# Expert passes in another order, and a context mixer's output turns and closing norms moved into the stages after the experts

## What is computed

```python
# end of the first block: 32 experts (4 groups of 8, top 2 of one group), then the final norm
x = x + gt2 * hier_moe(modulate(rms_norm(x, norm2_g), sh2, sc2), ...)   # w_gate, w_up, w_down: 3 x 2 MB each
x = rms_norm(x, final_norm_g)
# second block, layer 0: a mixer over latent and context; only the context starts before x is known
hx = rmsnorm(x, g_pre[0]) * (1 + scale) + shift
hc = rmsnorm(ctx, g_pre[0]) * (1 + scale_c) + shift_c
yx, yc = mlstm_pool_mixer(hx, hc, w_in, ..., w_out)      # yc needs hc only, yx needs the context's states
x   = x   + gate   * rmsnorm(yx, g_post[0])
ctx = ctx + gate_c * rmsnorm(yc, g_post[0])
# layer 1: window attention, needs the normed x and the normed ctx
```

## Time and profile before

| | |
|---|---|
| median of 3 runs | 1808.34 us (1799.67 to 1808.34) |
| profiled execution, its own time | 1805.27 us |
| its span | 1803.5 us |
| mean granted PE clock | 0.922 |
| PE busy | 1586.6 us, 88% |
| moved by DMA | 397.57 MB, mean 220 GB/s |
| first expert load issued, last expert step done | 566.8 us, 1184.6 us |
| first matmul of the latent's mixer (L1362) | 1245.0 us |

### The profile page before, as it was taken

How to read it: one execution, slowest core, us unless ns; L and a number is a source line. 1 busy time by engine, 2 the same in 40 slices (tenths; PEclk the granted TensorE clock), 3 DMA queues, 4 the chain that set the end, 5 groups by cost and what they waited for, 6 DMA issues and landing times.

```text
span 1803.5 us, 21928 instructions
## 1 busy us (share of the span) xinstructions
PE 1586.6 (88%) x9261; PEld 1078.5 (60%) x9261; DVE 488.0 (27%) x1222; ACT 339.2 (19%) x698; POOL 4.1 (0%) x8
## 2 busy tenths in 40 slices
PE   5799949898988878997998999976889999979797
PEld 2555649777877334453455664455676685867566
DVE  2200164541224241122213100024343231020581
ACT  2211230112121111202110001023112122121371
POOL 0000000000000000000000000000000000000000
PEclk9999966799978989998999999986899999989999
DMA  9577750132224989999999999951313313322000
GB/s 346 218 297 280 297 245 1 47 123 113 94 96 170 421 333 370 399 398 419 403 409 410 411 419 405 384 210 36 140 47 140 135 52 140 144 100 103 38 1 24
DMA packets 54304, 397.57 MB, mean 220 GB/s; under 512 B 6360, under 2 KB 13689, under 8 KB 16441
## 3 DMA queue, kind: packets, MB, share of 16 engines
q1 hardware_dynamic: 40384, 341.85, 47.4%
q10 hardware_dynamic: 13240, 52.16, 7.3%
q0 software_dynamic: 576, 2.10, 0.3%
HBM read 389.80 MB, written 6.29 MB: 220 GB/s over the span
## 4 chain that ended last, share of the span: by engine, by line
PE 76%; DMA 8%; DVE 8%; ACT 4%; issue 2%; PEld 1%; SPq 0%; ACTq 0%; PEldq 0%; DVEq 0%
PE bank L660 14%; PE bank L1373 12%; PE bank L1388 8%; PE bank L2300 6%; DMA work<-in_moe_w_up 4%; PE bank L2317 4%; PE bank L1488 3%; PE bank L1493 3%; PE bank L518 2%; PE bank L2286 2%; PE bank L689 2%; PE bank L1095 2%; PE bank L1083 2%; PE bank L840 1%; DMA work<-in_ab_pool_w 1%
## 5 line engine op out<-in xcount | busy, mean ns | idle before, releaser
L660 PE MATMUL bank<-H,ring 128*128 128x256 f32 (+1 forms) x928 | 244.4, 424 | 18.2 <-DVEq L294 8.2
L660 PEld LDWEIGHTS bank<-H,ring 128*128 128x128 f32 x928 | 178.8, 194 | 78.4 <-issue 49.3
L2300 PE MATMUL bank<-ring,work 128*32 128x512 f32 (+1 forms) x768 | 142.8, 656 | 19.2 <-DMA work<-in_moe_w_up 10.4
L1373 PE MATMUL bank<-H,work 128*128 128x256 f32 x512 | 116.7, 387 | 0.3 <-issue 0.3
L1373 PE MATMUL bank<-H,ring 128*128 128x256 f32 x512 | 112.9, 381 | 0.0
L1373 PEld LDWEIGHTS bank<-H,work 128*128 128x128 f32 x512 | 97.7, 193 | 19.6 <-issue 6.4
L1373 PEld LDWEIGHTS bank<-H,ring 128*128 128x128 f32 x512 | 98.1, 192 | 13.6
L2300 PEld LDWEIGHTS bank<-ring,work 128*32 128x32 f32 (+1 forms) x768 | 37.2, 126 | 111.9 <-issue 87.8
L1388 PE MATMUL bank<-work,H 128*128 128x512 f32 x192 | 85.2, 597 | 0.0
L1388 PE MATMUL bank<-ring,H 128*128 128x512 f32 x192 | 83.0, 592 | 0.0
L2317 PE MATMUL bank<-ring,work 128*32 128x512 f32 (+1 forms) x384 | 66.9, 611 | 2.8 <-issue 2.2
(11 more groups left out here) (403 smaller groups left out, 2010.5 us busy)
## 6 DMA issues: line engine op xcount, KB each, us to landing
ring<-in_moe_w_gate SPq DMA_DIRECT2D x48, 1024.0 KB, 11.6
ring<-in_moe_w_up SPq DMA_DIRECT2D x48, 1024.0 KB, 9.6
ring<-in_moe_w_down SPq DMA_DIRECT2D x48, 1024.0 KB, 12.1
work<-in_ab_w_in ACTq DMA_DIRECT2D x28, 1024.0 KB, 10.2
ring<-in_ab_w_in SPq DMA_DIRECT2D x14, 2048.0 KB, 7.5
ring<-in_ada_w SPq DMA_DIRECT2D x12, 2048.0 KB, 7.6
ring<-in_w_in SPq DMA_DIRECT2D x12, 2048.0 KB, 7.5
ring<-in_w_mod SPq DMA_DIRECT2D x12, 2048.0 KB, 7.7
```

Of the source, the lines that this page charges most:

```text
L660: mm = nc.tensor.matmul(bank[i % NB][:, 0:n], weight(c, k, j * P, (j + 1) * P), rhs(k), start=(k == 0), stop=(k == kt - 1))
L1373: mm = nc.tensor.matmul(b[:, j * T:(j + 1) * T], w_k(m, n, k, at, at + P), H[:, k, m.s], start=(k == 0), stop=(k == DT - 1), skip_group_ch ...
L2300: mm = nc.tensor.matmul(bank[b][rows, :], gath[:, k, rows], half_slot[(load_at[n + half] + e) % NHALF][:, (k % 4) * 512:(k % 4 + 1) * 512] ...
```

## The change

- `PASSES` becomes a list at the top: the four passes of two experts first, then the six of four. `start` takes 6 pieces in place of 4; `FILL_FOUR` goes from 16 pieces a pass to 13 with other places, `FILL_TWO` from 2 to 3.
- `out_pe`, `out_act`, `out_dve` take a list of turns. Turn 0 stays in the body (`OUT_EARLY`), turns 1 to 3 go to last1 (`OUT_LATE`). For the context they no longer write squares; `mixers[0].yo` moves to the end of `work`.
- last1 computes both norms of the latent at once: squares of X and of X times `final_norm_g`, two sums on PE, the second root from the first, two spreads, and DVE writes H for the mixer from X directly. The pre norm at the head of mix is gone.
- The context's two closing norms go to mix: `post` around the O rows of heads 0 and 1, `next` around the K tiles of heads 2 and 3.
- `moe_ring_free` is raised by 2 at the last step, and SP waits for the stores of all passes before it loads the latent's first weights.

```diff
-        PASSES = [(N_WIDE + 4 * i, 4) for i in range((NX - N_WIDE) // 4)] + [(2 * i, 2) for i in range(N_WIDE // 2)]
+PASSES = [(2 * i, 2) for i in range(N_WIDE // 2)] + [(N_WIDE + 4 * i, 4) for i in range((NX - N_WIDE) // 4)]
...
-                    self.yo = flat_tiles(self.pp, DT, T)
+                    self.yo = work[:, WORK - DT * T:WORK].rearrange("p (n t) -> p n t", t=T)
...
+        OUT_EARLY, OUT_LATE = (0,), (1, 2, 3)
-        FILL_FOUR, FILL_TWO = (2, 2, 2, 2, 2, 2, 2, 1, 1), (0, 0, 0, 1, 0, 1, 0, 0, 0)
+        FILL_FOUR, FILL_TWO = (2, 1, 1, 1, 2, 2, 1, 2, 1), (0, 0, 1, 1, 0, 0, 0, 1, 0)
...
-            for _ in range(4):
+            for _ in range(6):
                 next(body, None)
...
-                if p == NPASS - 1:
-                    nc.vector.sem_inc(moe_ring_free, 1)
-                else:
+                if p < NPASS - 1:
                     take_gathered(p + 1)
...
                 if p == NPASS - 1:
-                    nc.vector.sem_inc(moe_ring_free, 1)
+                    nc.vector.sem_inc(moe_ring_free, 2)
...
-            yield from out_pe(pe, m)
-            yield from norm_steps_pe(pe, m)
-            yield from norm_steps_pe(pe, m)
+            yield from out_pe(pe, m, OUT_EARLY)
...
         def last1_pe(pe):
+            out = out_pe(pe, mixers[0], OUT_LATE)
...
-            norm_pe(pe, H, T)
+            take(out, 2)
...
+            for i, src in enumerate((sq_x, sq_g)):
+                for k in range(DT):
+                    pe.wait_ge(sq_ready, DT * (u + i) + k + 1)
+                    for j in range(4):
+                        mm = nc.tensor.matmul(bank[i][32 * j:32 * j + 32, 0:64], ones[:, 0:32], src[:, k, j * 64:(j + 1) * 64],
...
+            take(out, 2)
...
+            for i in range(2):
+                pe.wait_ge(rinv_done, u + i + 1)
...
+            finish(out)
...
         def last1_dve(dve, chain):
...
+            finish(out_dve(dve, mixers[0], OUT_LATE))
+            dve.wait_ge(a_mm, turns["dve_a"])
+            dve.wait_ge(rstd_mm, STD_BEFORE[u + 1])
             for k in range(DT):
...
+                V.scalar_tensor_tensor(out=H[:, k, 0:T], in0=X[:, k, 0:T], scalar=coef[:, 0, k:k + 1], in1=bank[3][:, 0:T],
+                                       op0=ALU.mult, op1=ALU.mult).then_inc(scaled, 1)
+            for k in range(DT):
+                V.scalar_tensor_tensor(out=X[:, k, 0:T], in0=X[:, k, 0:T], scalar=vec("fng", k, k + 1), in1=bank[2][:, 0:T], op0=ALU.mult, op1=ALU.mult)
...
         def mix_pe(pe):
...
-            finish(norm_steps_pe(pe, m))
+            post = norm_steps_pe(pe, mixers[0])
+            after = norm_steps_pe(pe, mixers[0])
...
+            next(post)
             finish(rows_pe(pe, m, O[0]))
+            finish(post)
...
             finish(tiles_pe(pe, m, Q[1]))
+            next(after)
             finish(tiles_pe(pe, m, K[1]))
+            finish(after)
...
+            for i in range(2):
+                sp.wait_ge(rows_stored[i], 16 * (NPASS // 2))
             for j in range(len(second)):
                 load_chunk(sp, AT_SECOND + j)
```

More of the change, by code:

```diff
@@ L1479, in pool_pe, with out_pe @@
                 yield
-        def out_pe(pe, m):
-            for r in range(4):
+        def out_pe(pe, m, rs=range(4)):
+            for r in rs:
                 w_wait(pe, m, OUT[r])
@@ L1630, in pg_act, with out_act @@
             yield from tiles_act(act, m, PG[c], lambda act, m, b, pair: sil_act(act, m, b, 2 * c + pair), split)
-        def out_act(act, m):
-            for r in range(4):
+        def out_act(act, m, rs=range(4)):
+            for r in rs:
                 yield
@@ L1904, in pg_dve, with out_dve @@
                 yield
-        def out_dve(dve, m):
-            for r in range(4):
+        def out_dve(dve, m, rs=range(4)):
+            for r in rs:
                 yield
@@ L2686, in build, with take @@
         accT_mm, accT_out = sem("accT_mm"), sem("accT_out")
-        x_first = sem("x_first")
+        sq_x = hrows.rearrange("p t d -> p (t d)").rearrange("p (k t) -> p k t", t=T)
+        sq_g = work[:, WORK - 2 * DT * T:WORK - DT * T].rearrange("p (k t) -> p k t", t=T)
+        fused = sem("fused")
+        def take(steps, n):
+            for _ in range(n):
+                next(steps, None)
         def last1_pe(pe):
+            out = out_pe(pe, mixers[0], OUT_LATE)
             for j in range(DT):
@@ new lines, in last1_pe @@
+            take(out, 2)
+            norm_use["pe"] += 2
+            for i in range(2):
+                pe.wait_ge(rinv_done, u + i + 1)
+                for j in range(4):
+                    mm = nc.tensor.matmul(bank[2 + i][:, j * 64:(j + 1) * 64], bc(ident[:, 32 * j:32 * j + 1], [P, P]), rstd[:, (u + i) % 2, 0:64],
+                                          start=True, stop=True, skip_group_check=True)
+                mm.then_inc(rstd_mm, 1)
+            finish(out)
+        def last1_act(act, chain):
+            m = mixers[0]
+            out = out_act(act, m, OUT_LATE)
+            for k in range(DT):
+                act.wait_ge(accT_out, k + 1)
+                nc.scalar.activation(sq_x[:, k, :], X[:, k, 0:T], ACT.Square).then_inc(sq_ready, 1)
+            for k in range(DT):
+                nc.scalar.activation(sq_g[:, k, :], X[:, k, 0:T], ACT.Square, scale=vec("fng", k, k + 1)).then_inc(sq_ready, 1)
+            u = norm_use["act"]
+            norm_use["act"] += 2
+            act.wait_ge(sumsq_done, STD_BEFORE[u])
+            nc.scalar.activation(rstd[:, u % 2, 0:64], bank[0][:, 0:64], ACT.Sqrt, bias=epsc[:], scale=1.0 / D).then_inc(std_done, 1)
+            take(out, 4)
+            act.wait_ge(fused, 1)
+            nc.scalar.activation(rstd[:, (u + 1) % 2, 0:64], rstd[:, (u + 1) % 2, 0:64], ACT.Sqrt, bias=epsc[:]).then_inc(std_done, 1)
+            finish(out)
+            modulate_act(act, mod2, 0, (0,))
@@ new lines, in last1_dve @@
+            u = norm_use["dve"]
+            norm_use["dve"] += 2
+            r, g = rstd[:, u % 2, 0:64], rstd[:, (u + 1) % 2, 0:64]
+            dve.wait_ge(std_done, STD_BEFORE[u])
+            V.reciprocal(r, r).then_inc(rinv_done, 1)
+            dve.wait_ge(rinv_done, u + 1)
+            dve.wait_ge(sumsq_done, STD_BEFORE[u + 1])
+            L(V.scalar_tensor_tensor(out=g, in0=bank[1][:, 0:64], scalar=1.0 / D, in1=r, op0=ALU.mult, op1=ALU.mult))
+            V.tensor_tensor(g, g, r, ALU.mult).then_inc(fused, 1)
@@ L2751, in mix_act @@
             act.dma_start(m.pool_inv, d["pool_inv"]).then_inc(pool_in, 16)
-            finish(next_act(act, m, x_first, 0, mod2, 0))
+            post = post_act(act, mixers[0])
+            after = next_act(act, mixers[0], x_new, 0, mod2, 24)
             gate_in_act(act, m)
@@ L2774, in mix_dve @@
             wide_from.update(dve_d=turns["dve_d"])
-            finish(next_dve(dve, chain, m, vec("gpre", 0, 8), mod2, 8))
+            post = post_dve2(dve, chain, mixers[0])
+            after = next_dve(dve, chain, mixers[0], vec("gpre", 8, 16), mod2, 32)
             ones_dve(m)
@@ L2792, in mix_dve @@
             finish(heads_dve(dve, m, 0))
-            for c in range(4):
-                conv_dve(dve, chain, m, 4 + c)
+            for c in (4, 5):
+                conv_dve(dve, chain, m, c)
+            next(after)
+            for c in (6, 7):
+                conv_dve(dve, chain, m, c)
+            finish(after)
             a_seen(2)
```

50 lines of the change are left out of this document (26 added, 24 removed).

## The result

The changed kernel takes 1820.54 us (median of 6 runs, 1816.93 to 1826.12), beside 1806.57 us (1799.67 to 1810.46) for the kernel before on the same chip: ratio 1.0084, 95% interval 1.0056 to 1.0112. It is slower, by 10 to 20 us. Its profiled execution took 1817.44 us (span 1815.5), against 1805.27 us (span 1803.5) of the earlier trace rows.

What follows compares the result with a forecast made beforehand. DMA was taken as the nearer limit in the experts' stage, PE as full in the latent's mixer. Gates' start +0.9, gates -1.0 and mix +9.3 make +9.2 on 1805.27: 1814.5 us, range 1797 to 1829.

Steps and rivals of the forecast that it cites:

- The experts' stage: First expert load to last expert step: 15.2 us of weights, 12 of holes and 6 of tail go, 33 us in all.
- A: Rival: in the experts' stage the DMA holes of 24.5 us close fully, 12.5 us more off, 1797.5 at most; chance 0.22.
- C: Rival: PE bounds the passes of four experts and no DMA holes close, +12, 1826.5 us in all; chance 0.13.
- 12 pieces (108 to 96): Experts' stage: PE loses three output turns, 12 pieces, 42 us of PE work.
- the holes: Experts' stage: transfers missing for 24.5 us in all, of which half, 12 us, was taken to close.
- The tail: End of the experts' stage: last load in to last step's end takes about 10 us instead of 15.6, 6 less.
- Four gate pieces and output turn 0: Behind the last expert step PE has these in a row, 14.0 and 14.1 us, until 1179.8.
- Taken as covered: Behind the experts: the fetch of their rows is in by the end of turn 0, 1179.8; bounds 0 and 7.6 us.
- The transposes now start 5.9 behind turn 0: Behind the experts: ACT's copy, 0.7, and 5.2 us from ACT's weighting to the transposes put their start at 1185.7.
- last1: Transposes to the latent's gates: PE work of 51.9 us, then 8.3 for DVE's scalings and the drain; gates start at 1245.9.
- mix: Latent's mixer: two sums and two spreads, each sum behind ACT's squares, add 9.3 us on a full PE; bounds 4.7 and 12.
- Behind the closing sum: From the latent's closing sum to the end of the span: no difference predicted, 0.

Runs made afterwards that it cites:

- Before_half: The kernel before with half the bytes of every expert weight loaded and that half read by the experts' matmuls; experts' stage 571.0 us in one run.
- after_half: The changed kernel with half the bytes of every expert weight loaded; experts' stage 527.7 us in one run.
- after_fours: The changed kernel with the passes of four experts first again, same fill tables; ratio to the kernel before 1.024.
- ring_later: The changed kernel, but SP starts the second ring loads only when the fetch of the experts' rows has landed; ratio to the kernel before 1.0113.
- squares_early: The changed kernel with ACT's squares for the two context norms in the latent's mixer issued one section earlier; ratio to the kernel before 1.0066.
- scale_later: The changed kernel with DVE's scaling of X moved from ahead of the latent's gates to the head of mix; ratio to the kernel before 1.007.
- two_cover: The changed kernel with output turns 0 and 1 ahead of the transposes and only turns 2 and 3 behind; ratio to the kernel before 1.0114.
- all_together: The changed kernel with early squares, early weighting and late ring loads, later X scaling, three gate pieces in the last pass, later ACT weight loads; ratio to before 1.0055.
- gates_inside: The changed kernel with early squares, early weighting, later X scaling and ACT weight loads, all gate pieces before the last expert step, two turns before the transposes; ratio 1.003.

## Why the prediction came out as it did

Forecast 1814.5 us, range 1797 to 1829; measured 1820.54, inside. The side I had thought likeliest, within 0.5%, is not what came: the ratio's whole interval lies above 1.005, a case with a chance of 0.37. Against the sum's own reference the forecast was 2.9 us low (1817.44), but 4.8 us of luck ahead of the first expert load hide that it was 7.7 low. By its steps:

- **The experts' stage, -33.** Right in mechanism and nearly in size: -35.4, last step at 1144.4 (1149.2 if the stage began as before) for 1151.7. A (1139) and C (1164) are out. Before_half and after_half show that transfers set the length. The parts of the sum are less sure than the sum. "12 pieces (108 to 96)" and "33 of the 42 us" miss the four gate pieces, which the next step itself puts behind the stage: up to the last expert step it is 108 to 92. By the prediction's own measure the holes shrank from 24.5 to (1.01 - 0.98) / 1.01 x 582.4 = 17 us, 7 and not 12, though a share given to 0.01 makes that uncertain by some 6 us; after_fours shows that it depends on which pieces meet which pass, for with the fours first the share is 0.95. The tail gave 4 us and not 6: before, the last load was issued at 1162.5 and took 11.0 to land, so that it was in at about 1173 and not 1169, 11 us ahead of the last step's end; now it is about 7. And PE does not wait for the last 4 MB, as "come in with PE waiting" has it: from 1120 to the last step's end it is busy without a gap.
- **"Four gate pieces and output turn 0", 28.1.** Failed: I put turn 0 right behind the gates, and its first operand is the product of the last gate tile. 2.37 us.
- **"Taken as covered", the fetch.** Failed, within its bounds of 0 to 7.6: it landed 3.9 us behind turn 0, 27.9 behind its first issue. Nearest was the bound that lets all 10.5 MB go together, 25.4 us. The Trainium skill's round robin (DMA: Bandwidth & Descriptors, "Queues, rings and completion order") had given an estimate of 17; 2.1 MB in 27.9 us are 75 GB/s, 0.18 of the rate and not 0.30. The other weight queue was beside it, as that step had warned.
- **"The transposes now start 5.9 behind turn 0".** Failed at 9.4. The fetch's 2.0 of waiting is in it, but ring_later shows that the gap does not go away with the fetch: ACT issues the next weight load before it copies (1.2), and the drain depends on DMA. The term was copied from a row where DMA was idle.
- **last1, 60.2 to the gates.** 59.0. Right, to 1.2 us, but the end was counted too long: 8.3 for DVE's two scalings and the drain, and 6.5 measured. DVE ends at 1243.14 and PE starts at 1243.22. The 1.6 us of drain had come from the way out of the experts' branch, and this stage has no branch to leave. And the 1 us taken off the gates did not come: they took 6.39, with the clock at 0.57.
- **mix, +9.3.** +10.7 (11.0 without the 0.3 of the gates). The two sums are as forecast in all (3.3 and 3.5 from PE free to sum done, 3.5 and 3.6 said), though most of it is the sum itself and not the wait; the spreads take 1.0 each. The other 1.8 is in the K tiles behind the second sum, which take 15.77 us after PE's wait for squares, and 14.08 in squares_early, where that wait is gone.
- **Behind the closing sum, 0.** +2.9, with no edit there: one group of 64 matmuls (L677 before, L676 after) takes 15.55 us before and 17.07 after, the last spread 1.10 and 1.97. Over that group the granted clock is 0.90 before and 0.82 after (the two make up 2.4 of the 2.9 us); why these places were hit was not tried.

## What to carry to other kernels

In a stage that transfers bound, PE work taken out gives back less than its length (35.4 us for 51.6 here), and it costs its full length in a place where PE is the limit: before moving it out, halve the bytes and see what the stage needs without them. That does not make work put in free: three pieces (10.5 us) lengthened the stage by 11.5 us and four (14 us) by 18.8. In the first case the trace shows PE standing 7.2 us at a piece whose weights had just been asked for; in the second the cause stays open. And the last pieces in the stage are also the cover of what follows. A gap behind a stage should be read to its last releaser: removing the wait that the profile names (the fetch) moved nothing, since the next in line (the way out of a branch, slowed by the very loads that had been put off) took its place.

## What the runs showed of the hardware

- The way out of a branch costs more the busier DMA is: from DVE's last operation to PE's first in the next stage 1.6 us (before, DMA share 0.00 over it), 1.86 to 2.21 (changed kernel, squares_early and scale_later, 0.07 to 0.10), 2.80 (two_cover, 0.45), 4.25 (ring_later, 0.84) and 4.27 (all_together, 0.75). PE starts 1.5 to 1.8 us after the last packet of q14 ahead of it is in. Between last1 and mix, where there is no branch, it is 0.08 us.
- A fetch of 2.1 MB by POOL took 9.9 us with no ring loads beside it (ring_later, all_together), 27.9 beside 8.4 MB on two other queues, and 32.7 in after_fours.
- A PE wait of 6.5 us brought the granted clock to 0.57 for the next 6.4 us. One of 3.9 us left it at 1.00 in scale_later and brought it to 0.68 over the next 5.4 us in all_together and gates_inside, though PE was busy at 1.00 ahead of it in all three.
